# Layer 0's input projection as seven block products per chunk in place of eight

## The reference, cut to what matters

```
hcat = x @ w_in                       # (256 x 1024) @ (1024 x 2048)
u, q, k, v = split(hcat, 4)           # 512 columns each
y_pool = pool_mixer(u)                # trailing means over 2/4/8/16 tokens, then a 128x128 product per group
y_sb   = stick_breaking(q, k, v)      # 8 heads of 64
out    = concat(y_pool, y_sb) @ w_out
```

## Time and profile before

| | |
|---|---|
| Time, median of 3 runs | 1316.38 us (1316.04 to 1316.53) |
| Profiled execution, its own time | 1317.43 us |
| Its span, first to last instruction | 1315.7 us |
| Mean granted TensorE clock | 0.997 |
| PE busy | 1298.4 us (99%) |
| DVE busy | 437.3 us (33%) |
| ACT busy | 262.0 us (20%) |
| POOL busy | 80.9 us (6%) |

### The profile page before, as it was taken

How to read it: one execution, slowest core, us unless ns; L and a number is a source line. 1 busy time by engine, 2 the same in 40 slices (tenths; PEclk the granted TensorE clock), 3 DMA queues, 4 the chain that set the end, 5 groups by cost and what they waited for, 6 DMA issues and landing times.

```text
span 1315.7 us, 23435 instructions
## 1 busy us (share of the span) xinstructions
PE 1298.4 (99%) x9788; PEld 753.6 (57%) x9788; DVE 437.3 (33%) x960; ACT 262.0 (20%) x522; POOL 80.9 (6%) x125
## 2 busy tenths in 40 slices
PE   9999999999999999999999999999999999999997
PEld 8889444435534443549688998834444353444533
DVE  2145122222312222228664665422223132222313
ACT  1232211111111111113432330211111111111111
POOL 7302000000000000000002201100000000000001
PEclk9999999999999999999999999999999999999999
DMA  5698799999999999996542016799999999999995
GB/s 180 167 380 324 304 421 419 422 422 422 422 405 422 422 421 422 422 399 192 180 161 99 4 38 269 312 384 418 422 422 422 422 410 417 422 421 422 422 422 214
DMA packets 98823, 450.38 MB, mean 342 GB/s; under 512 B 16192, under 2 KB 45504, under 8 KB 49088
## 3 DMA queue, kind: packets, MB, share of 16 engines
q1 hardware_dynamic: 98752, 449.34, 85.0%
HBM read 448.26 MB, written 1.05 MB: 342 GB/s over the span
## 4 chain that ended last, share of the span: by engine, by line
PE 94%; DVE 3%; SPq 1%; DMA 1%; ACT 1%; issue 0%; POOL 0%; DVEq 0%; POOLq 0%
PE PS L1964 31%; PE PS L2006 17%; PE PS L2014 10%; PE PS L1935 7%; PE PS L538 4%; PE PS L500 3%; PE PS L1426 2%; PE PS L1451 2%; PE PS L1412 2%; PE PS L1978 2%; PE PS L1986 1%; PE PS L1605 1%; PE PS L1589 1%; PE PS L2021 1%; PE PS L2093 1%; DMA RING<-in_ab_w_out 1%
## 5 line engine op out<-in xcount | busy, mean ns | idle before, releaser
L2324 DVE TENSOR_TENSOR y_parts<-PS,y_parts 128x512 fp32r<-128x512 f32 x128 | 88.6, 692 | 216.7 <-ACT y_parts L2226 216.7
L2298 DVE SCALAR_TENSOR_TENSOR AR<-AR,PS 128x256 f32<-128x256 f32 x64 | 30.8, 481 | 380.5 <-ACT AR L2204 380.5
L2014 PE MATMUL PS<-y_parts,token_map 128*128 128x512 f32 x496 | 143.2, 415 | 0.0
L2014 PEld LDWEIGHTS PS<-y_parts,token_map 128*128 128x128 f32 x496 | 84.6, 188 | 61.3 <-issue 49.4
L2006 PE MATMUL PS<-AR 128*64 128x512 f32 x512 | 116.9, 598 | 0.0
L2006 PE MATMUL PS<-RING,AR 128*64 128x512 f32 x384 | 116.8, 598 | 0.0
L2226 ACT CAST y_parts<-PS 128x512 fp32r<-128x512 f32 x128 | 75.1, 586 | 171.9 <-PE PS L2006 171.9
L1964 PE MATMUL PS<-RING,xT 128*64 128x512 f32 x480 | 108.2, 592 | 0.4 <-issue 0.4
L1964 PE MATMUL PS<-AR,xT 128*64 128x512 f32 x480 | 108.2, 592 | 0.3 <-issue 0.3
L1964 PE MATMUL PS<-AR 128*64 128x512 f32 x480 | 108.1, 592 | 0.0
L1964 PE MATMUL PS<-RING,AR 128*64 128x512 f32 x480 | 108.1, 592 | 0.0
(11 more groups left out here) (332 smaller groups left out, 1548.1 us busy)
## 6 DMA issues: line engine op xcount, KB each, us to landing
RING<-in_moe_w_gate SPq DMA_DIRECT2D x64, 1024.0 KB, 11.3
RING<-in_moe_w_up SPq DMA_DIRECT2D x64, 1024.0 KB, 13.4
AR<-in_moe_w_gate SPq DMA_DIRECT2D x64, 1024.0 KB, 12.5
AR<-in_moe_w_up SPq DMA_DIRECT2D x64, 1024.0 KB, 14.5
AR<-in_moe_w_down SPq DMA_DIRECT2D x64, 1024.0 KB, 13.3
RING<-in_moe_w_down SPq DMA_DIRECT2D x48, 1024.0 KB, 14.1
GB<-in_moe_w_down SPq DMA_DIRECT2D x16, 1024.0 KB, 14.8
AR<-in_ab_w_in SPq DMA_DIRECT2D x16, 512.0 KB, 4.6
```

The source lines that it names most:

```text
L2014: ins = nc.tensor.matmul(PS[:, 2 * t + h, :], OHT[:, half, t, :], YS[:, n, h * 512:(h + 1) * 512], start=False, stop=True, skip_group_chec ...
L2298: nc.vector.scalar_tensor_tensor(out=HH[0:2 * B, :].rearrange("p (k j) -> p k j", k=FT), in0=by_row(SIL[0:2 * B, :]), scalar=GC[:, buf:buf ...
L2324: nc.vector.tensor_tensor(YS[:, 1, h * 512:(h + 1) * 512], PS[:, 5 + h, :], YS[:, 0, h * 512:(h + 1) * 512], ALU.subtract).then_inc(q["low ...
```

## The change

Each chunk's product (256 tokens x 1024 channels) @ (1024 x 256) is seen as a 2x2 by 2x2 block product and computed by Strassen's scheme in Winograd's form: seven block products instead of eight. A block product is four matmuls of 128x128 weights and 128 moving columns. The sums of input blocks (four, once) and of weight blocks (four for each chunk) are made by VectorE, both inputs in SBUF. Partial results go through PSUM, are copied to SBUF by ScalarE (four 128x128 copies a chunk) and are combined by VectorE (four 128x128 sums a chunk). The loops over chunks are unrolled.

```diff
+        def pe_blocks(pe, c):
...
+            pe.wait_ge(s_wl[c % 2], 16 * (c // 2 + 1))
+            product(x_block(0, 0), w_block(c, 0, 0), 0, True).then_inc(s_pj, 1)
+            pe.wait_ge(s_wr[c % 2], 16 * (c // 2 + 1))
+            product(x_block(0, 1), w_block(c, 1, 0), 1, True).then_inc(s_pj, 1)
+            pe.wait_ge(s_ws, sums(c, 1))
+            product(S1, t1, 2, True).then_inc(s_pj, 1)
+            pe.wait_ge(s_ws, sums(c, 2))
+            pe.wait_ge(s_part, 4 * c + 1)
+            product(S2, t2, 0, False).then_inc(s_pj, 1)
+            pe.wait_ge(s_ws, sums(c, 3))
+            pe.wait_ge(s_part, 4 * c + 2)
+            product(S4, w_block(c, 1, 1), 2, False).then_inc(s_pj, 1)
+            pe.wait_ge(s_c0, 2 * c + 1)
+            product(x_block(1, 1), t4, 1, True).then_inc(s_pj, 1)
+            pe.wait_ge(s_ws, sums(c, 4))
+            pe.wait_ge(s_part, 4 * c + 3)
+            product(S3, t3, 0, False).then_inc(s_pj, 1)
```

```diff
-            v.wait_ge(s_const, 2)
-            nc.vector.reciprocal(ICN[:, :, :], ICN[:, :, :]).then_inc(s_l0c, 1)
...
+            v.wait_ge(s_xT, 4)
+            for n in range(4):
+                dve_token_sum(v, link, n)
+                dve_weight_sum(v, 0, n)
...
+            for c in range(8):
+                if c == 6:
+                    masked(0)
+                elif c == 7:
+                    stick_weights(0)
+                dve_block(v, c, 0, 0)
+                if c < 7:
+                    for n in range(4):
+                        dve_weight_sum(v, c + 1, n)
+                dve_block(v, c, 0, 1)
+                if c == 6:
+                    running_product(0)
+                dve_block(v, c, 1, 0)
+                dve_block(v, c, 1, 1)
+                if c == 1:
+                    v.wait_ge(s_const, 2)
+                    nc.vector.reciprocal(ICN[:, :, :], ICN[:, :, :]).then_inc(s_l0c, 1)
```

More of the change, by code:

```diff
@@ L231, in program @@
         assert a0_.at <= AFL - 9 * P
+        blocks = Area(flat, 0, 6144)
+        XSUM = blocks(4, 4, P)
+        WSUM = blocks(2, 4, 4, P)
+        PART = WT[:, 0:4, :]
         a0b = Area(flat, 12288, 18432)
@@ L470, in load_chunk @@
                 sp.dma_start(chunk(b)[:, ks, :], src[:, ks, ds(c * CB, CB)]).then_inc(loaded, 16)
[L472 to L483, removed]
@@ L485, in swapped @@
         def swapped(x):
             return x.rearrange("p (t a r) -> p t a r", t=TT, a=2)[:, :, ::-1, :]
[L489 to L525, removed]
@@ L542, in project_out @@
                     ins.then_inc(s_res, 1)
[L544 to L548, removed]
         def constants(g):
@@ L643, in program, with sums @@
         w_out = a["ab_w_out"][0].rearrange("(k p) c -> p k c", p=P)
+        def sums(c, n):
+            return 2 * n if c == 0 else 4 + 4 * c + n
         def sp_mix0(sp):
@@ L702, in by_head, with x_block, w_block, weight_sums @@
             return m[:, 0:H0 * (keys(q) + 1)].rearrange("p (h k) -> p h k", h=H0)
+        S1, S2, S4, S3 = [XSUM[:, n, :, :] for n in range(4)]
+        def x_block(t, kh):
+            return xT[:, 4 * kh:4 * kh + 4, t * P:(t + 1) * P]
+        def w_block(c, kh, f):
+            return chunk(c % 2)[:, 4 * kh:4 * kh + 4, f * P:(f + 1) * P]
+        def weight_sums(c):
+            return [WSUM[:, c % 2, n, :, :] for n in range(4)]
+        def region(c, n):
+            return PS[:, (1, 5, 1, 5, 1, 5, 5, 1)[c] + n, 0:P]
@@ new lines, in out_block, with product @@
+        def out_block(c, t, f):
+            if c < 6:
+                return UQK[:, 2 * c + f, t * P:(t + 1) * P]
+            return V0[:, t, (c - 6) * CB + f * P:(c - 6) * CB + (f + 1) * P]
+        def pe_blocks(pe, c):
+            t1, t2, t4, t3 = weight_sums(c)
+            def product(x, w, n, start):
+                for k in range(4):
+                    sides = (w[:, k, :], x[:, k, :]) if c < 6 else (x[:, k, :], w[:, k, :])
+                    ins = nc.tensor.matmul(region(c, n), *sides, start=(start and k == 0), stop=(k == 3),
+                                           skip_group_check=True)
+                return ins
+            if c == 6:
+                pe.wait_ge(s_pe, 4 + 2 * 6)
+            elif c == 7:
+                pe.wait_ge(s_zm, 4)
+            pe.wait_ge(s_wl[c % 2], 16 * (c // 2 + 1))
[15 more added lines that the diff above has]
+            product(S3, t3, 0, False).then_inc(s_pj, 1)
@@ new lines, in act_part @@
+        def act_part(s, c, n):
+            if n == 0:
+                if c:
+                    s.wait_ge(s_c0, 2 * c - 1)
+                s.wait_ge(s_pj, 7 * c + 1)
+            elif n == 1:
+                s.wait_ge(s_pe, 4 + 2 * c)
+                s.wait_ge(s_pj, 7 * c + 3)
+            elif n == 2:
+                s.wait_ge(s_pj, 7 * c + 4)
+            else:
+                s.wait_ge(s_pj, 7 * c + 7)
+            nc.scalar.copy(PART[:, n, :], region(c, (0, 2, 0, 0)[n])).then_inc(s_part, 1)
@@ L710, in pe_mix0 @@
             pe.wait_ge(s_xT, 4)
-            project_channels(pe, xT, 0, 6, 0)
+            for c in range(6):
+                pe_blocks(pe, c)
             def scores(q):
@@ L745, in heads @@
                                                start=(k == 0), stop=(k == q))
-                ins.then_inc(s_o, 1)
+                ins.then_inc(s_att, 1)
             scores(0)
-            project_tokens(pe, xT, 6, 2, 12)
+            for c in range(6, 8):
+                pe_blocks(pe, c)
             scores(1)
@@ L779, in act_mix0 @@
                 copy_turned(s, nc.scalar.copy, 0, n)
-            s.wait_ge(s_xT, 4)
-            copy_tiles(s, UQK, 0, 3)
+            for c in range(6):
+                for n in range(4):
+                    act_part(s, c, n)
+            act_part(s, 6, 0)
             def turned(q):
-                s.wait_ge(s_wt, q + 1)
+                s.wait_ge(s_att, TURNED[q])
                 for n in range(2 * q + 2):
```

119 lines of the change are left out of this document (88 added, 31 removed).

## The result

| | before | after |
|---|---|---|
| Time, median of 4 runs | 1316.21 us (1315.40 to 1316.53) | 1328.70 us (1327.19 to 1329.68) |
| Profiled execution, its own time | 1317.43 us | 1328.13 us |
| Its span | 1315.7 us | 1326.4 us |
| Mean granted TensorE clock | 0.997 | 0.994 |
| TensorE: matmul records, busy | 9788, 1298.4 us | 9980, 1295.5 us |

The kernel became slower: the ratio is 1.0094, 95% interval [1.0081, 1.0107]. TensorE's busy time fell by 2.9 us, and yet the span grew by 10.7. The page's part 4, the chain that ended last, says where to look: TensorE's share fell from 94% to 93%, and GpSimd, which had none, has 2%.

What follows compares the result with a forecast made beforehand. TensorE was taken to bound the kernel, at 94% of the chain. Second scores at 76.7 against 65.2 gave +11.5, less 0.5 for `w_out`; 1317.43 + 11.0 - 1.05 = 1327.4 us, range 1319.5 to 1332.5.

Steps and rivals of the forecast that it cites:

- A: The forecast case for the changed stage: gate and a late GpSimd, 1323.5 to 1331 us, chance 0.60.
- G: Delay of GpSimd's constants by VectorE's 16 early sums with two SBUF inputs: 6.0 us taken, bounds 0 and 8.8.
- The gate: Product 6 of chunk 2 waits for VectorE's block sum behind the reciprocal, which waits for GpSimd's constants: 34.15 us at earliest.
- Rival B: The gate alone, GpSimd's single-input instructions not held or only now and then: 1319.7 to 1323.4 us, chance 0.24.
- The clock: TensorE's clock falls to half after the idle time ahead of product 6 of chunk 2: 1.7 us lost, bounds 0 and 3.4.
- The products: In the changed stage a 128-column matmul costs 0.2245 us, a chunk 6.29 against 6.95: 5.3 us saved over eight.
- Rival C: Not slower: 128-column matmuls in this stream cheaper than in the shared expert, 0.202 us each needed; chance 0.08.
- GpSimd's window sums beside the weight sums: After the gate, in chunks 3 and 4, they hold VectorE: 0 to 2 us, taken as 0.
- Rival D: More lost: VectorE late in chunks 3 and 4, or 56 new waits cost 0.1 us each; 1332 to 1336 us, chance 0.08.
- ScalarE in chunk 6: Its second copy stands behind a table load and a sigmoid, so product 5 comes late: 0.4 us with the hand-off.
- The wait for `w_out`: TensorE's wait of 0.50 us at 75.94 us goes away, as the weight comes earlier against TensorE: 0.5 us less.
- One for one behind the stage: Whatever the new stage adds or saves up to the second scores goes into the total one for one.

Runs made afterwards that it cites:

- the fillers: The changed kernel with 48 filler products, results unused, between products 5 and 6 of chunk 2, inside TensorE's idle time: 1324.98 us.
- the reordered kernel: The late and short one, with chunk 0's first block sum ahead of its last two input sums and ScalarE's chunk 6 copies ahead of sigmoids: 1314.54 us.
- the short reciprocal: The changed kernel with GpSimd writing the constant columns as 1/window and the reciprocal over 16 columns, in its old place: 1320.74 us.
- two waits: The reordered kernel with two more long-fulfilled waits ahead of each of TensorE's 56 block products: 1311.34 us.
- the late and short one: The changed kernel with the reciprocal over 16 columns, the others written by GpSimd, and moved from behind chunk 1 to behind chunk 3: 1315.01 us.
- the one with the eighth product: The reordered kernel with an eighth product of four 128-column matmuls in every chunk, result not used: 1318.51 us.
- the run with one wait: The reordered kernel with one more long-fulfilled wait ahead of each of TensorE's 56 block products: 1313.49 us.
- the late reciprocal: The changed kernel with the full reciprocal and its wait moved from behind chunk 1 to behind chunk 3: 1320.27 us.

## Why the prediction was right

It said 1327.4 (range 1319.5 to 1332.5), slower, by A; measured were 1328.70. Term by term, to the second scores:

| Step | Forecast | Measured |
|---|---|---|
| constants ready, then reciprocal starts (27.2 + G) | 33.2 | 31.76 |
| reciprocal and block sum | 6.95 | 6.75 |
| product 6 of chunk 2 | 40.15 | 38.51 |
| from there to the end of chunk 5, low clock included | 22.4 | 23.34 |
| first scores | 1.16 | 1.09 |
| chunks 6 and 7 | 13.0 | 13.28 |
| second scores | 76.7 | 76.22 |
| against before | +11.5 | +11.0 |

The closeness is in part luck: in these rows the constants came 1.4 us sooner than forecast and the low clock cost 1.0 more, so that they nearly cancel, and behind the stage two terms that the forecast did not have cancel too (last point).

- **The gate.** Right, and its mechanism is shown: without the reciprocal no idle time. The idle time of 12.03 us lies in the 8 to 16 named.
- **GpSimd's delay G.** The mechanism is right, and shown by the operand moved to PSUM; the size was 4.5 instead of 6.0, thus 0.28 us a sum instead of the 0.55 that gave the upper bound of 8.8 (or the 0.375 in the 6.0). Rival B's premise, that single-input GpSimd instructions are not held, is refuted: the selections took 2.00 us instead of 1.38.
- **The clock.** It fell, as said, but the term was too small: 1.7 taken, 2.6 measured against the fillers' full clock (half of the 5.5 us at half clock gives 2.7), inside the bounds of 0 and 3.4. The row that it was taken from the earlier trace rows had a pause of 0.6 us; here the clock was at half from 30.3 us (the window at 30, at 0.58) to 44, for 8 us of idle time and 5.5 us of work behind it.
- **The products.** 0.2235 us a matmul, against 0.2245. Rival C needed 0.202. A chunk is 6.26, not 6.29. Yet the whole stage saves 4.4 us at best, in the reordered kernel and counted from the first product, against the 5.3 forecast: its chunk 0 takes 7.04 us (7.99 to 15.03), not 6.26. The forecast let the stage start at 8.48 as before; it starts at 8.08.
- **GpSimd's window sums beside the weight sums** were taken at 0, and cost 0 here: chunk 4 takes 6.26 us (49.25 to 55.51) like those behind it, though single weight sums took up to 2.19 us. Rival D is refuted for this kernel; with full clock behind the gate (the fillers) it costs 0.27.
- **ScalarE in chunk 6** cost 0.34 us of idle time, near the 0.4 forecast; from start to start the two products ahead of it take 2.30 us (64.83 to 67.13) in place of 1.79, so 0.5. The wait for `w_out` went away: the router of layer 0 starts at 115.25 against 105.01, +10.24, where 11.0 was forecast after it; that is 0.76 given back instead of 0.5. This cannot be counted on: the kernels with the short reciprocal and with two waits waited 1.50 and 1.90 us there.
- **"One for one behind the stage"** is the step that did not hold fully. Two terms were missing that nearly cancel. The idle times at the head of layer 1 add 2.3 us (a lag of 606.42 - 596.06 = 10.36 becomes 619.08 - 606.40 = 12.68). Then 2.0 are given back by the end, where the span is 10.7 longer: the kernel before has its stretch at low clock at 770 us, which cost it 1.7 by its windows, while all of the kernel after's windows from 764 to 794 us stand at 1.00. One of them:

```profile
770.00:776.00 6.00, 6.00 (x230) 6.00 (x228) 3.40 (x6) 1.17 (x2) 0.00 (x0) 1.00 0.01 3
```

  Such stretches come and go between these kernels: the reordered one has one at 734 us, the kernel after, the late and short one, the one with the eighth product and the one with two waits have none in layer 1. Neither term could be read from the profile of before as an effect of this change. The profiled executions differ by 1328.13 - 1317.43 = 10.7, against the 11.0 forecast; the medians by 12.5. The 1.05 us that was taken off for the profiled execution of before did not carry over: the one of after lies 0.57 under its own median.

The causes of the idle times at the head of layer 1 stay open. Shown, by one profile of each kernel, is that they come, go and move with how much code of TensorE stands ahead, most plainly by the run with one wait: two in the kernel after, the reordered one and those with the late, the short, and the late and short reciprocal; one small one (0.50 us, a little later) with the fillers; none at these places with the eighth product, with two waits, and in both kernels with eight long products. That the engine waits there for its own instructions would fit, as the profile names no semaphore; no run shows it, and none was made that moves the code without changing TensorE's program.

## What to carry to other kernels

Saving matmuls by giving VectorE work between them turns VectorE's whole program into TensorE's program: before such a change, look for everything long or waiting in that stream (here one reciprocal of 6.55 us behind a wait for GpSimd) and place it by its due time, not by where it happens to stand. The same seven products are 0.94% slower or 0.12% faster, and the difference is made by one line moved, one instruction shortened and two hand-offs reordered; with a longer program it is 0.40%, of which a part stays unexplained. And price the pieces in the size in which they will run: an eighth less arithmetic was worth 4.4 us of the stage's 56.7 and not 7, since a matmul with half the columns costs more than half and the first chunk has to wait for its parts.

## What the runs showed of the hardware

- A matmul of float32 with 128 moving columns takes 0.2235 us back to back, one with 256 columns 0.434: two of the short ones cost 13 ns, or 3%, more than a long one. The Trainium skill ("TensorE: Matmul & The Clock Gate", Wait — 56ns, not 53.3ns?) states a fixed cost of about 2.5 ns for each matmul at full clock; the sign agrees, and whether the size does, no run here shows.
- Sixteen VectorE sums with two SBUF inputs made GpSimd's constants 4.5 us late, though most of what GpSimd did had a single input. The held instruction's waiting time is inside its duration in the trace (2.00 us for two selections of 1.38), and no idle time points to it.
- A reciprocal of 128x1024 float32 takes 6.55 us on VectorE, of 128x64 0.55: (6.55 - 0.55)/960, or 6.3 ns for each further element of the free size. A two-input sum of 128x512 takes 0.68 us, 1.3 ns an element.
- After an idle time of 3.09 us TensorE's clock was at 0.50 too, and not at once: in the kernel with the late reciprocal the window at 42 us, when it works again, stands at 0.86 and the next at 0.50. After 3.52 us of idle time, in the kernel with the short reciprocal, the window in which it works again, at 30 us, already stands at 0.51.

```profile
42.00:44.00 2.00, 1.94 (x15) 1.94 (x16) 1.90 (x3) 0.00 (x0) 2.00 (x1) 0.86 0.73 252
44.00:46.00 2.00, 2.00 (x11) 2.00 (x11) 1.97 (x3) 0.27 (x1) 1.92 (x3) 0.50 0.00 0
```
